# Turning the expert down table: a third output buffer, the next load ahead of the stores, and another spread of the turns

## What is computed

```python
def first_block(x, ...):
    xn = rmsnorm(h, mix_norm_w)
    proj = xn @ w_in
    y_a = pool_mixer(xa, pool_w, pool_scale) @ w_pool_up
    y_b = deltanet_branch(qkv, z, beta_logit, a_logit, ...) @ w_dn_up   # conv, 8 heads, chunked delta rule
    merged = sigmoid(gate_a) * y_a + sigmoid(gate_b) * y_b
    h = h + merged @ w_mix_out
    h = h + peer_ffn(rmsnorm(h, ffn_norm_w), ...)   # 8 heads pick 16 of 128*128 experts for each token
...
def peer_ffn(x, w_query, keys_1, keys_2, expert_down, expert_up):
    ...
    u = take(expert_down, experts)                   # rows of a 16384 x 1024 table
    act = gelu(einsum("btd,bthkd->bthk", x, u))
    v = take(expert_up, experts)
    return einsum("bthk,bthkd->btd", gates * act, v)
```

## Time and profile before

| | us |
|---|---|
| median of 3 runs | 2973.29 |
| lowest, highest run | 2971.91, 2978.59 |
| profiled execution | 2982.77 |
| its span | 2980.8 |
| PE busy | 2726.0 (91% of the span) |
| DVE busy | 1890.5 (63%) |
| DMA moved | 569.90 MB, mean 191 GB/s |

### The profile page before, as it was taken

One profiled execution on the slowest core, in us unless ns is written; L12 is line 12 of the kernel. 1 busy time (PEld: TensorE's weight loads), 2 busy tenths in 40 slices (PEclk: granted clock), 3 DMA queues, 4 the chain that ended last, 5 costly groups with the idle time before them and its releaser, 6 DMA issues. The chain is left out here.

```text
span 2980.8 us, 39136 instructions
## 1 busy us (share of the span) xinstructions
PE 2726.0 (91%) x13559; PEld 2290.7 (77%) x13559; DVE 1890.5 (63%) x3324; ACT 1111.3 (37%) x1670; POOL 877.1 (29%) x768
## 2 busy tenths in 40 slices
PE   6998888979887899888999999999979999999998
PEld 5677777667676888767899999999967777766887
DVE  5785455544477888455877777788863683545334
ACT  4443233323222677322333333333344333454222
POOL 1012334100033777202444444555520030033000
PEclk8999999999999899999999999999989999999999
DMA  4656655376255344799999998999932212200332
GB/s 144 219 186 191 184 162 175 115 246 214 109 176 179 134 170 167 244 322 317 344 317 315 317 324 290 322 310 316 321 129 92 71 36 78 85 8 31 104 99 85
DMA packets 250560, 569.90 MB, mean 191 GB/s; under 512 B 23600, under 2 KB 138416, under 8 KB 248752
## 3 DMA queue, kind: packets, MB, share of 16 engines
q1 hardware_dynamic: 208400, 406.72, 41.7%
q0 software_dynamic: 36864, 134.23, 12.7%
q10 hardware_dynamic: 5152, 27.11, 2.4%
HBM read 468.89 MB, written 99.09 MB: 191 GB/s over the span
## 5 line engine op out<-in xcount | busy, mean ns | idle before, releaser
L230 DVE TENSOR_TENSOR split<-raw,split 128x1024 fp32r<-128x1024 f32 x368 | 450.1, 1224 | 496.7 <-ACT split L221 496.4
L221 ACT ACTIVATE split<-raw 128x1024 fp32r<-128x1024 f32 x424 | 447.2, 1055 | 787.8 <-PE up L1564 205.0
L1562 PE MATMUL up<-split,weight_high 128*128 128x512 f32 x768 | 305.1, 397 | 33.3 <-DVE weight_low L2541 27.2
L1564 PE MATMUL up<-split,weight_low 128*128 128x512 f32 x768 | 304.9, 397 | 0.0
L1563 PE MATMUL up<-split,weight_high 128*128 128x512 f32 x768 | 304.8, 397 | 0.0
L272 DVE STREAM_TRANSPOSE turn<-turn 128x1024 f32<-128x1024 f32 x128 | 158.5, 1241 | 229.4 <-DMA turn<-in_stream 228.7
L1837 POOL DMA_INDIRECT picked_rows<-down_rows,picked x128 | 185.0, 1445 | 338.2 <-DVE picked_rows L2550 173.7
L1837 POOL DMA_INDIRECT picked_rows<-in_stream,picked x128 | 204.0, 1594 | 207.2 <-DVE acc L2559 181.6
L1562 PEld LDWEIGHTS up<-split,weight_high 128*128 128x128 f32 x768 | 146.7, 191 | 68.7 <-issue 40.5
L245 PE MATMUL query<-xh,split 128*128 128x384 f32 (+1 forms) x384 | 152.2, 396 | 20.7 <-POOL split L230 20.4
L1564 PEld LDWEIGHTS up<-split,weight_low 128*128 128x128 f32 x768 | 146.6, 191 | 31.5
(11 more groups left out here) (522 smaller groups left out, 6535.0 us busy)
## 6 DMA issues: line engine op xcount, KB each, us to landing
raw<-in_stream SPq DMA_DIRECT2D x440, 512.0 KB, 5.2
turn<-in_stream SPq DMA_DIRECT2D x128, 512.0 KB, 5.2
down_rows<-turn SPq DMA_DIRECT2D x512, 128.0 KB, 4.0
gates<-stage ACTq DMA_DIRECT2D x12, 2048.0 KB, 7.3
gate<-gates SPq DMA_DIRECT2D x30, 768.0 KB, 7.7
h<-in_x SPq DMA_DIRECT2D x4, 512.0 KB, 5.9
h<-in_x SPq DMA_DIRECT2D x1, 2048.0 KB, 8.0
h_saved<-h SPq DMA_DIRECT2D x1, 2048.0 KB, 7.6
```

The source lines that it names most:

```text
L221: act.activation(g.high[t % slots], g.raw[:, t % RAW, :], ACT.Copy).then_inc(g.high_split, 1)
L230: dve.tensor_tensor(g.low[t % slots], g.raw[:, t % RAW, :], g.high[t % slots], ALU.subtract).then_inc(g.low_split, 1)
L1562: pe.matmul(bank, xh, hi[:, w], start=start, stop=False, skip_group_check=True)
L1564: return pe.matmul(bank, xl, hi[:, w], start=False, stop=stop, skip_group_check=True)
```

## The change

The output has three buffers in place of two (the last pair of heads keeps two), so a turn waits for the store of the turn three before. SP no longer stores first: a new function `move` waits for the turn, issues the load two turns ahead, and then stores. It stands in the step of SP's list that belongs to the turn's own step. In delta both loads of a level come first, each behind its turn, then both stores, and the raw load of level 6 behind them. The turns are spread differently: conv 22 (from step 0 on, DVE's turn now in the step of its own number), delta 12, 12, 12 and 8, merge 22 (from step 2 on), query 16, early 24, which is 128 again. `FIRST_DOWN` goes from 5 to 7 and `SPREAD` from (7, 7, 6) to (7, 6, 5): two more down tiles stand before pick tile 0, one fewer in each of pick tiles 1 and 2. POOL's first pool window moves from the second pair of heads to the third.

```diff
-TURN_CONV, TURN_DELTA, TURN_MERGE, TURN_QUERY, TURN_EARLY = 20, 48, 20, 16, 24
+TURN_CONV, TURN_DELTA, TURN_MERGE, TURN_QUERY, TURN_EARLY = 22, (12, 12, 12, 8), 22, 16, 24
...
-        self.stored = [g.sem(f"turn_stored{k}") for k in range(2)]
+        self.stored = [g.sem(f"turn_stored{k}") for k in range(3)]
...
-    def turn(self, dve, n, tile, out):
+    def turn(self, dve, n, tile, out, lag=3):
         dve.wait_ge(self.loaded[n % 2], 16 * (n // 2 + 1))
-        if n >= 2:
-            dve.wait_ge(self.stored[n % 2], 64 * (n // 2))
+        if n >= lag:
+            dve.wait_ge(self.stored[(n - lag) % 3], 64 * ((n - lag) // 3 + 1))
...
+    def move(self, sp, n, out, upto, tile):
+        sp.wait_ge(self.turned, n + 1)
+        if n + 2 < upto:
+            self.load(sp, n + 2, tile)
+        self.store(sp, n, out)
...  # conv, SP
-                    n = p - 4
+                    n = p - 2
                     if 0 <= n < TURN_CONV:
-                        turner.store(sp, n, conv_out[n % 2])
-                        if n + 2 < TURN_CONV:
-                            turner.load(sp, n + 2, conv_in[n % 2])
+                        turner.move(sp, n, conv_out[n % 3], TURN_CONV, conv_in[n % 2])
...  # delta, SP
-                        for e in range(2):
-                            ...
-                            turner.store(sp, n, delta_out[k][n % 2])
-                            if i + 2 < per_pair:
-                                turner.load(sp, n + 2, delta_in[k][n % 2])
+                        turns = turns_at(k, lv)
+                        for n in turns:
+                            sp.wait_ge(turner.turned, n + 1)
+                            if n + 2 < turn_from[k + 1] or k < 2:
+                                turner.load(sp, n + 2, ...)
+                        for n in turns:
+                            turner.store(sp, n, delta_out[k][n % len(delta_out[k])])
+                        if lv == LEVELS - 1 and k < 3:
+                            load_next(N_CONV + 3 + 3 * k + 2)
...  # conv, DVE
-                    if 0 < j <= TURN_CONV:
-                        turner.turn(dve, j - 1, conv_in[(j - 1) % 2], conv_out[(j - 1) % 2])
+                    if j < TURN_CONV:
+                        turner.turn(dve, j, conv_in[j % 2], conv_out[j % 3])
...  # merge, DVE (turn_first = 2)
-                    if p < turns:
-                        turner.turn(dve, turn_from + p, turn_in[p % 2], turn_out[p % 2])
+                    filled = turn_from + p - turn_first
+                    if turn_from <= filled < turn_from + turns:
+                        turner.turn(dve, filled, turn_in[filled % 2], turn_out[filled % 3])
...  # merge, query and early, SP: the same with n = p - 4, p - 3, x - 3 for p - 3, p - 4, x - 4
-FIRST_DOWN = 5
+FIRST_DOWN = 7
-SPREAD = (7, 7, 6)
+SPREAD = (7, 6, 5)
```

More of the change, by code:

```diff
@@ L654, in delta_front, with turns_at @@
     turner = g.turner
[L655 to L659, removed]
+    conv_in, conv_out = turner.buffers((R + 46, R + 48)), turner.buffers((R + 50, R + 52, R + 54))
+    delta_in = [turner.buffers((R + 63, R + 10))] * 3 + [turner.buffers((R + 24, R + 32))]
+    delta_out = [turner.buffers(pages) for pages in (
+        (R + 4, R + 6, R + 8), (R + 20, R + 22, R + 28), (R + 22, R + 24, R + 32), (R + 26, R + 34))]
+    turn_from = [TURN_CONV + sum(TURN_DELTA[:k]) for k in range(HEADS // 2 + 1)]
+    def turns_at(k, lv):
+        n = TURN_DELTA[k]
+        return range(turn_from[k] + n * (lv - 1) // (LEVELS - 1), turn_from[k] + n * lv // (LEVELS - 1))
     def per(b):
@@ L1195, in _ @@
                         part(h + 1, lv)
-                    if k == 1:
+                    if k == 2:
+                        turner.landed(pool, turn_from[2])
                         pool.wait_ge(m["k_normed"], 4)
@@ L1353, in _ @@
                             split_low(g, dve, 0, N_CONV + tiles[1] + 2)
-                        for e in range(2):
-                            n = TURN_CONV + per_pair * k + 2 * (lv - 1) + e
-                            turner.turn(dve, n, delta_in[k][n % 2], delta_out[k][n % 2])
+                        for n in turns_at(k, lv):
+                            turner.turn(dve, n, delta_in[k][n % 2], delta_out[k][n % len(delta_out[k])], 3 if k < 3 else 2)
                         if lv == LEVELS - 1 and k < 3:
@@ L1479, in _ @@
                 for n in range(min(turns, 2)):
-                    turner.load(sp, turn_from + n, turn_in[n % 2])
+                    turner.load(sp, turn_from + n, turn_in[(turn_from + n) % 2])
                 for p in range(len(tiles) + RAW):
                     stream_load_each(g, sp, p + 1, p)
[L1483 to L1487, removed]
+                    n = turn_from + p - 2 - turn_first
+                    if turn_from <= n < turn_from + turns:
+                        turner.move(sp, n, turn_out[n % 3], turn_from + turns, turn_in[n % 2])
                 sp.wait_ge(rows, 16)
@@ L3489, in build @@
         g.run(merge, (g.ph, g.pl), len(POOL_WINDOWS), (g.yh, g.yl), io["x"], READY, R + 4,
-              tuple(R + 20 + 4 * c for c in range(6)), turns=TURN_MERGE, turn_pages=(R + 20, R + 22, R + 24, R + 26))
+              tuple(R + 20 + 4 * c for c in range(6)), turns=TURN_MERGE, turn_pages=(R + 20, R + 22, R + 24, R + 26, R))
         g.run(mix_out_norm, "ffn_norm", R)
```

72 lines of the change are left out of this document (32 added, 40 removed).

## The result

The changed kernel takes 2882.82 us (median of 4 runs, 2877.39 to 2889.88), against 2975.94 for the kernel before (median of 4 runs). The ratio is 0.9684, with an interval of 0.9662 to 0.9707: about 93 us faster. The forecast was 2875, range 2835 to 2926.

A forecast was written before the change was run, and what follows sets the result against it. Late turn loads were taken to hold DVE and so PE. Conv +2.5, delta -34, merge -24, query -26, pick -7, early -10 sum to -98.5: 2884.3 on the profiled execution, 9.5 above the median, so 2875; range 2835 to 2926.

The forecast's parts named there:

- What bounds it: In delta, merge, query and early, a turn's late load holds DVE, which holds PE; gaps also bring half clock.
- Merge and query: PE's waits for low splits and lost clock shrink: merge -24 of at most 33.6, query -26 of at most 34.3.
- Early: Third buffer and earlier load let nearly full DMA engines run without pauses: -10 us, ends -3 and -33.
- Delta: Shorter levels (26 us) and half the wait for the state (8): -34 us, ends -8 and -60.
- the price of the levels: In delta, 12 level intervals fall from 9.4 to 7.2 us, as packets should be shorter: 26 us.
- the wait for the state: In delta, PE's 15.4 us wait for the recurrence's state, from the last level's turns; half goes, 8 us.
- the third buffer covers the stores behind both loads: In delta, storing behind both loads delays the first turn's store; the third buffer covers it except in the last pair.
- R3: Rival, chance 0.08: DVE's wait moves from load to store, as SP issues stores late; about half remains, -49, so 2924.
- R1: Rival, chance 0.2: the DMA engines bound delta and early, which give only 8 and 3; -65.5, so 2908.
- Pick: Two more down tiles fill PE's 8.75 us gap before tile 0: 10.9 at most, less 4.3 for POOL splits, -7.
- Conv: Two added turns of 1.25 us each, taken in full as PE is nearly always busy: +2.5; 0 if they hide.
- S: Rival, slower, chance 0.04: DMA engines limit all four stretches, no wait goes, only added work remains; +10.8, about 2984.

The follow-up runs named there:

- the halved stores: Two kernels: turn by turn in delta, plus delta and early stores halved in bytes or in number; delta shorter by 14.9 and 11.7 us, early by 18.9 and 23.1.
- the two other runs with this delta: Changed kernel with SP reaching turns one step later outside delta (2929.75 us), and changed kernel with the down tiles as before (2878.42 us).
- Turn by turn: Changed kernel, but in delta SP does wait, load and four stores for each turn, instead of both loads then eight stores: 2868.62 us, ratio 0.9620.

## Why the prediction was right, and where its terms were off

*What bounds it: right.* A load issued late holds DVE and DVE holds PE. (One reading of the earlier trace rows was wrong: the state's 15.4 is PE's sixth largest wait, behind 18.1 in the scores for which the page names no engine. Nothing here rests on it.) The step shows it: put back by one step, the waits of PE return in merge, query and early; with nothing but the step, nearly all of their gain is there. The prediction also gave weight to issuing the load ahead of the stores and to the third output. In merge, query and early neither brings more than 4 us once the step is right.

*Merge and query: too small by 9 and 6.* I left a fifth of merge's waits, a third of its lost clock and a quarter of query's sum. In fact nearly all of it went; the ceilings that stood there, 33.6 and 34.3, were nearly the answers (32.8 and 31.7). Two steps of lead covered the load completely, at a DMA share of 0.93 in merge.

*Early: too small by 10.* The room up to a share of 1.03, 18 us, was the right figure, and I took half of it. The stage gained 19.7 and stands at 1.00. That the stores' traffic sets it is shown by the halved stores: PE then fills nearly all of the stretch or all of it (133.13 of 136.10, 131.90 of 131.90).

*Delta: -18.8 instead of -34.* The crosses of levels 3 and 6 of the second pair, after:

```profile
318.02 2.07 PE L831 MATMUL front<-kn,db 128*128 128x128 f32 x16
...
340.87 2.07 PE L831 MATMUL front<-kn,db 128*128 128x128 f32 x16
```

That is 22.9 for three intervals, against 26.7 in this pair before. The step that failed is the price of the levels, 12 intervals from 9.4 to 7.2. They took 107.4 us together before, 9.0 each, as the one pair I read was the slowest of the four. After, they take 95.1, or 7.9 each, so 12 came of the 26 (15 or 16 in the two other runs with this delta).

The reason given for 7.2, shorter packets, came only in small part: the engines' busy time for each MB in delta (DMA share over GB/s, so an estimate from rounded figures) went from 3.35 us to 3.25, some 3%, where going from 8.6 to 7.2 asks for 16. Of the wait for the state 5.1 went (15.4 to 10.3) where I let 8 go.

The sentence that the third buffer covers the stores behind both loads was wrong: the first turn's stores wait for the second turn, and the wait for loads turned into one for stores. That is R3's outcome, in this stage alone, though not by R3's time to issue: the turn at 398.15 was done at 399.40, and until 402.92 SP waited for the second turn. Turn by turn the stage gains 10.7 more, which is most of the missing 15. Of what remains, the stores' bytes or packets set 12 to 15, which is R1's side.

The second thing I had not priced is the spread. Four turns fewer in the last pair bring 10.5, and without them the new order and the third output together bring only some 8 here. The turn by turn order was not run with the old spread, so whether the two gains add is open.

*Pick: 0 instead of -7.* The price of the two splits beside the selection was right, 4.2 where I had 4.3. The gain was not: half of the gap stayed (4.18 of 8.75), with the half clock behind it, and of the 10.9 at most only 4.2 came, the time from the turn of tile 0 to the end of pick (252.5 before, 248.3 after). The end named there (given back, 0) came true; that DVE sets the rest of pick is argued from its share there, not shown by a run.

*Conv: 0 instead of +2.5.* The two turns do cost that, 3.0 by the run with the old spread, but the rest of conv's change gave as much back: with 20 turns and the new order conv takes 172.1, against 175.6 before. What in it did so is not shown: with the step late conv takes 174.8, with the old order and two outputs 175.9, so it needs neither the step by itself nor order and third output; the turn's earlier place on DVE's list was not tried apart. The wait at its start grew from 2.56 to 3.69, as the prediction said it might.

The errors cancelled: merge, query and early gave 24 us more than forecast, delta, pick and conv together 19 less, and the rest varied by 4. That the whole came out within 8 us of the forecast, with most stages off by 6 to 15, is partly luck. S did not come near: no stage with turns got slower.

## What to carry to other kernels

- When an engine's in-order list carries a side job, look at when the job's loads are issued, before adding buffers: one step earlier was worth 78 us here by itself (of the 99.8 between the two profiled executions) and 51 on top of the other parts. The third buffer mattered in delta alone, and there with both loads ahead of the stores (25.5), not with the stores first (2.1, within the spread).
- If two items of a side job fall into one step, let each be stored as soon as it is done. Grouping loads ahead of stores put one item's store behind the other's wait, and that came back as a wait one step on. Within one item, issue the load ahead of its stores where a load has little time: in delta that order was worth 17.4.
- After a wait is gone, ask each stage for its next bound in numbers: PE busy in merge and query, the stores' traffic in early and part of delta. Where the next bound lies well beyond, take the whole wait.

## What the runs showed that I had not expected

Early became shorter when each turn waited longer. With a wait for the store two back it took 145.6 us at 365 GB/s and 148.5 at 360 GB/s, with three back 151.1 to 155.0 (352 GB/s in the changed kernel):

```profile
1170.50:1316.10 145.60, 136.56 (x576) 110.74 (x577) 102.74 (x130) 49.15 (x65) 12.22 (x10) 0.96 1.02 365
```

With the wait two back and the stores first it took 152.4, so the order plays a part. These are single profiles of each kernel, and the cause was not settled.
